# A hybrid encoder step on one core: the order of the transfers at the seam into the mixing stage, and the product W = T X in alternating column tiles

## The chip, the cores and the metric

The kernel runs on one core of a Trainium2 chip. It is written for the engines directly: each engine (TensorE or PE for matmuls, VectorE or DVE, ScalarE or ACT, GpSimd or POOL, SyncE or SP, which here only issues DMAs) has its own list of instructions and runs it in order. The engines meet at semaphores alone. The metric is the time of one execution on the device in microseconds (us); less is better.

## The reference, cut to what matters

One layer for 1024 prompt rows and 32 sample rows of width 1024. The part that the change touches:

```
h = RMSNorm(x);  p = h @ w_in          # q/kv latents, rwkv columns z, gate logits (2*D_MODEL)
branch A: multi-head latent attention over chunks
branch B: zm = z + (prev - z) * mu;  r, k, v, decay, a, g from zm
          per step: s = s*w + (s a) b + v k;  y = s r      # delta rule, 8 heads of 64
x = x + sum_n sigmoid(gate_n) * (branch_n @ w_out[n])
x = x + HierMoE(RMSNorm(x))            # top-1 of 4 groups, top-2 of 8 experts, 32 experts in all
outputs also: kv latents, rope keys, the state, the last projected row (shift)
```

## The kernel before, in words

The rows are cut into NT = 9 tiles of 128 (eight of the prompt, the ninth with the 32 sample rows). The stages follow each other: the inputs' projection (names a_), the mixing (b_, with some shared buffers r_), attention (c_), output projection and router (d_), experts (f_).

**Mixing.** The delta rule is solved in blocks: for each tile t and head, a triangular system is inverted by merging (levels 2 to 64; `low` and `merge`), giving T in `U`; then W = T X (`solved`), the new state (`state`) and the outputs (`outputs`). A loop over laps s = -1 to 9 runs three tiles at once in steps k = 0 to 11: features of tile s+1, the inverse of tile s, and right side, W, state and outputs of tile s-1. `solved(t)` stands at k = 2 of a lap.

Between these small pieces PE fills in the gate logits: 36 items q = 0 to 35, nine tiles for each of four column blocks, as 128x512 matmuls of `hT[q % 2]` and a weight block `wg[u % 2]` of 2 MB. How many go where is a table (`FILL_OF`). Six parts of item 0 run ahead of the turned heads of the last input tile. For each item q, SP stores the logits (`store_logits(q)`, after ACT copied them out of PSUM) and loads the `hT` of item q+2 into the buffer that item q has left (`load_hT(q + 2)`). So item 3 needs the load that follows `store_logits(1)` in SP's order.

**The seam.** SP's mixing list begins while the last input tile is still being stored. It loads `hT` 1 and `zm` 1; stores the last `zm` and turned heads, then the two last projected rows (`shift`, 128x14 elements of 4 bytes each); stores logits 0, loads `hT` 2; waits until all stores of the input stage have landed and tells POOL and DVE so (`inputs_over`); loads the second weight block `wg[1]`, which item 9 is the first to read; and copies rows of `x` into an unused part of `gate_d` (two copies in DRAM of 384 KB), to have numbers there. Only then come `store_logits(1)` and `load_hT(3)`.

**W = T X.** T has a left half of columns (rows 0 to 63 alone are not zero) and a right half. For the left one, PE runs eight matmuls on 64 rows of `U[t % 2]` into PSUM rows 0 to 63; then it waits for `lower_copied` and runs eight on all 128 rows of `U_right` into PSUM rows 64 to 127. ACT copies the lower part of `U_right` at k = 10 of the lap ahead (`copy_lower`); DVE writes its upper part. Each float32 matmul is two instructions in the trace.

The mixing's `state`, `outputs` and `right_side` are written so that a matmul for PSUM rows 0 to 63 and one for rows 64 to 127 follow each other in turn (`for q in HALVES`).

Of the kernel before, what the change touches and what calls it, by code (L numbers as in the profile page):

```python
# [23 lines left out]
ACT = mybir.ActivationFunctionType  # L24
AX = mybir.AxisListType.X

P = 128
# [101 lines left out]
def inputs_stage(nc, io, early, held, block):  # L129

    HK = H * QK // 2
    with ExitStack() as c:
# [68 lines left out]
        def store_zm(sp, t):  # L201
            sp.wait_ge(zm_ready, t + 1)
            sp.dma_start(io["zm_d"][t], zm[:]).then_inc(zm_stored, 16)
# [6 lines left out]
                    mm = pe.transpose(banks[b][0:QK, j * P:(j + 1) * P], qk[:, first + h + j, :], ident[:])  # L210
                mm.then_inc(qkT_done, 1)

        def store_last(sp):

            store_zm(sp, NT - 1)
            store_qk(sp, NT - 1)
            for g in range(2):
                sp.wait_ge(row_kept, g + 1)
                sp.dma_start(io["shift"][g], zlast[:, g, :]).then_inc(shift_stored, 16)

        def all_stored(sp):
# [8 lines left out]

        last = dict(sems=sems, over=inputs_over, mixed=(zm_ready, NT), z_copied=(z_copied, NG_Z * NT), z_done=(z_done, NG_Z * NT), zm_stored=(zm_stored, 16 * (NT - 1)),
                    kv_copied=(qkv_copied, turn(NT)), turned_copied=(qkT_copied, turns_before(NT)),
                    store=store_last, stored=all_stored, turn_heads=lambda pe: turn_heads(pe, NT - 1))

        @block.sync
        def _(sp):
# [381 lines left out]
def mixing(nc, io, early, held, inputs, hand_over, block):  # L618
# [10 lines left out]
    with ExitStack() as c:  # L629
# [42 lines left out]
        M = [sb(f"M{j}", [P, H, 2, 2 * P]) for j in range(2)]  # L672
        T = sb("T", [P, H, HALF_T])
        U = [sb(f"U{j}", [P, H, HALF_T]) for j in range(2)]
        U_right = sb("U_right", [P, H, HALF_T])
        ident64 = sb("ident64", [P, HALF_T])
        L = [sb(f"L{i}", [P, H, Q if i < 2 else HALF_T]) for i in range(4)]
# [25 lines left out]
        def after(eng, sem, n):  # L703

            if n > 0:
                eng.wait_ge(sem, n)
# [17 lines left out]
        def _(sp):  # L724
# [24 lines left out]
            load_hT(1)  # L749
            sp.wait_ge(*inputs["zm_stored"])  # L750
            load_zm(1)
            inputs["store"](sp)
            store_logits(0)
            load_hT(2)
            inputs["stored"](sp)
            load_wg(1)
            for n in range(2):
                sp.dma_start(io["gate_d"][LAST, DEC:, 2 * n:2 * n + 2, :], io["x"][LAST, DEC:, :].rearrange("p (a b) -> p a b", a=2)).then_inc(no_logits, 16)
            q = 1
            for s in range(-1, NT + 1):  # L760
                if s >= 2:
                    sp.wait_ge(out_ready, s - 1)
                    sp.dma_start(io["ob_d"][s - 2], y[:]).then_inc(ob_stored, 16)
                for _ in range(6):
                    if q < ITEMS and parts_upto(q + 1) <= fill_upto(s):
                        store_logits(q)
                        if q + 2 < ITEMS:
                            load_hT(q + 2)
                        if tile_of(q) == LAST and unit_of(q) + 2 < UNITS:
                            load_wg(unit_of(q) + 2)  # L770
                        q += 1
                if s + 3 < NT:
                    load_zm(s + 3)
                if s == LAST:
                    sp.wait_ge(bon_done, NT)
                    sp.wait_ge(v_turned, NT)
                    load_head(sp, io, early, 0, 0, early["head_in0"])
                    sp.wait_ge(state_out, 1)
                    sp.dma_start(io["wkv"][0], grown[:]).then_inc(state_stored, 16)
# [10 lines left out]
        @block.gpsimd  # L790
        def _(pool):
            pool.wait_ge(*inputs["z_done"])
            pool.memset(bias[:, 0:1], CENTRE)
            pool.memset(bias[:, 1:2], -CENTRE)
            pool.memset(one[:], 1.0).then_inc(set_done, 1)
            pool.wait_ge(inputs["over"], 1)
            pool.memset(L[2][:], 0.0)
            pool.memset(S[0][:], 0.0).then_inc(set_done, 1)

            pool.wait_ge(lora_done, 1)  # L800
            pool.wait_ge(v_copied, 1)
            pool.wait_ge(gram_copied, PAIRS)
            give_back(pool, inputs["sems"])
            prime(pool, next_ones)
# [198 lines left out]
        def _(act):  # L1003
# [59 lines left out]
            def copy_lower(t):  # L1063
                act.wait_ge(merged, NL * t + NL - 1)
                after(act, w_done, t)
                h = H // 2
                act.activation(U_right[HALF_T:, 0:h, :], U[t % 2][HALF_T:, h:, :], ACT.Copy)
                act.activation(U_right[HALF_T:, h:, :], U[t % 2][HALF_T:, 0:h, :], ACT.Copy).then_inc(lower_copied, 1)

# [59 lines left out]
        def _(pe):  # L1129
# [96 lines left out]
            def solved(t):  # L1226
                pe.wait_ge(x_copied, t + 1)
                pe.wait_ge(merged, NL * t + levels_of(t))
                pe.wait_ge(U_ready, TURNED * (t + 1))
                after(pe, y_copied, t)  # L1230
                for h in range(H):
                    cols = slice(h * RH, (h + 1) * RH)
                    mm = pe.matmul(banks[WY][0:HALF_T, cols], U[t % 2][0:HALF_T, h, :], X[0:HALF_T, cols], start=True, stop=True)
                if t < LAST:
                    pe.wait_ge(lower_copied, t + 1)
                    for h in range(H):
                        cols = slice(h * RH, (h + 1) * RH)
                        mm = pe.matmul(banks[WY][HALF_T:, cols], U_right[:, h, :], X[:, cols], start=True, stop=True)
                mm.then_inc(w_done, 1)

            def state(t):
# [1331 lines left out]
```

## Time and profile before

| | us |
|---|---|
| median of 3 runs | 1621.47 |
| lowest, highest | 1621.18, 1624.18 |
| the profiled execution | 1621.25 |
| its span, first to last instruction | 1619.4 |
| PE busy | 1498.9 (93%) |
| DVE busy | 857.0 (53%) |
| ACT busy | 445.2 (27%) |

The input stage takes the first 342 us, the mixing goes on to 898, attention to 1088, the output projection to about 1270, the experts to the end. A busy share is an average over stages with different limits; a wait of one engine costs only where the others wait for it in turn. DVE and ACT have idle time in all stages.

### The profile page before, as it was taken

How to read it: one execution, taken by the hardware profiler on the slowest of the kernel's cores; microseconds unless marked ns; L12 is line 12 of the kernel's file. 1: busy time of each engine (PE TensorE's matmuls, PEld its weight loads, DVE VectorE, ACT ScalarE, POOL GpSimd, SP SyncE). 2: the span in 40 equal slices, each digit the busy share in tenths (PEclk: the TensorE clock that was granted, in tenths of full speed). 3: DMA queues.
4: the chain of work that ended last, by engine and by line, in shares of the span. 5: the costliest groups of instructions: out<-in, count | busy, mean ns of one | idle time of the engine just before them, and what ended most of it. 6: DMA issues, size and time to landing. Idle time of an engine off the chain costs nothing. (4 is left out here: it accounts for less than half of the span.)

```text
span 1619.4 us, 38770 instructions
## 1 busy us (share of the span) xinstructions
PE 1498.9 (93%) x16352; PEld 1062.5 (66%) x16352; DVE 857.0 (53%) x1874; ACT 445.2 (27%) x882; POOL 102.1 (6%) x102
## 2 busy tenths in 40 slices
PE   6999999998999999999998699988999599999994
PEld 5888888864666666666666466653554477777772
DVE  3545554464666766767667566664767323222111
ACT  2222222241233233233231244434444211111110
POOL 0000000000000000000000000000000122233321
PEclk9999999998999999999999699998999699999998
DMA  9422221553142132211112434436963799999972
GB/s 334 177 91 97 90 91 64 197 176 127 60 130 89 63 114 74 78 65 66 60 59 63 117 84 91 91 75 249 371 217 130 277 316 338 343 352 359 349 242 45
DMA packets 101326, 259.55 MB, mean 160 GB/s; under 512 B 34240, under 2 KB 53328, under 8 KB 91824
## 3 DMA queue, kind: packets, MB, share of 16 engines
q1 hardware_dynamic: 93424, 239.92, 43.1%
q0 software_dynamic: 7744, 17.33, 4.5%
q8 instruction: 124, 2.03, 0.5%
q14 instruction: 34, 0.28, 0.0%
HBM read 205.32 MB, written 60.56 MB: 164 GB/s over the span
## 5 line engine op out<-in xcount | busy, mean ns | idle before, releaser
L560 PEld LDWEIGHTS a_ps<-a_hT,a_wz 128*128 128x128 f32 x1792 | 202.6, 192 | 6.2 <-issue 3.8
L560 PE MATMUL a_ps<-a_hT,a_wz 128*128 128x128 f32 x1792 | 204.1, 275 | 1.7 <-DMA a_wz<-w_z 1.7
L1981 PE MATMUL d_ps<-late,last_down 128*128 128x512 f32 x256 | 115.4, 598 | 1.5 <-DVE last_down L1745 0.8
L2347 DVE TENSOR_SCALAR f_y<-f_down,table 96x512 f32<-96x512 f32 x32 | 23.9, 747 | 116.7 <-PE f_down L2142 68.0
L2149 DVE COPY f_xT<-f_turned 128x384 f32<-128x384 f32 x32 | 17.8, 557 | 128.0 <-PE f_turned L2116 128.0
L1981 PEld LDWEIGHTS d_ps<-late,last_down 128*128 128x128 f32 x256 | 46.7, 190 | 51.5 <-issue 50.2
L868 DVE TENSOR_TENSOR b_M<-b_ps,r_causal 128x512 f32<-128x512 f32 x72 | 46.4, 686 | 58.6 <-PE b_ps L1209 58.1
L1506 ACT ACTIVATE late<-c_score,c_top 128x1024 f32<-128x1024 f32 (+8 forms) x72 | 50.6, 703 | 92.7 <-DVE c_top L1455 92.2
L1146 PE MATMUL b_ps<-r_wg,b_hT 128*128 128x512 f32 x128 | 64.2, 627 | 5.2 <-DMA b_hT<-hT_d 5.2
L1146 PE MATMUL b_ps<-r_wg,r_hT 128*128 128x512 f32 x128 | 63.0, 625 | 2.0 <-DMA r_hT<-hT_d 2.0
L1146 PE MATMUL b_ps<-b_wg,b_hT 128*128 128x512 f32 x128 | 63.3, 616 | 0.7 <-DMA b_hT<-hT_d 0.7
L1146 PE MATMUL b_ps<-b_wg,r_hT 128*128 128x512 f32 x128 | 63.1, 615 | 0.0
L2142 PE MATMUL f_down<-wd,f_midT 128*96 128x512 f32 x136 | 61.3, 593 | 1.8 <-DVE f_midT L2161 1.8
L1299 PE MATMUL b_solve<-b_L,b_U 64*64 64x32 f32 x1408 | 57.2, 222 | 5.6 <-DVE b_L L944 5.4
L2354 ACT ACTIVATE f_xT<-f_turned 128x384 f32<-128x384 f32 x32 | 15.7, 491 | 163.9 <-PE f_turned L2116 163.9
L1299 PEld LDWEIGHTS b_solve<-b_L,b_U 64*64 64x64 f32 x1408 | 51.2, 136 | 13.5 <-DVE b_L L944 6.5
L472 ACT ACTIVATE a_z<-a_ps 128x512 f32<-128x512 f32 (+1 forms) x36 | 19.6, 544 | 140.9 <-PE a_ps L560 134.1
L944 DVE TENSOR_TENSOR b_L<-b_solve,r_merge_mask 128x256 f32<-128x256 f32 x44 | 18.7, 424 | 72.4 <-PE b_solve L1283 72.4
L1283 PEld LDWEIGHTS b_solve<-b_T,b_M 64*64 64x64 f32 x1408 | 44.5, 135 | 18.4 <-issue 7.8
L1553 PE MATMUL c_turned<-c_ident,late 128*128 128x128 f32 (+1 forms) x304 | 49.9, 290 | 6.1 <-ACT late L1506 6.1
L2266 POOL DMA_INDIRECT out<-f_y,rows x32 | 46.3, 1446 | 138.9 <-DVE f_y L2347 135.1
L2372 ACT ACTIVATE f_y<-f_down,table 96x512 f32<-96x512 f32 x32 | 21.9, 684 | 120.1 <-PE f_down L2142 70.8
(373 smaller groups left out, 2924.0 us busy)
## 6 DMA issues: line engine op xcount, KB each, us to landing
wgu<-w_gate_up SPq DMA_DIRECT2D x15, 2048.0 KB
late<-w_gate_up SPq DMA_DIRECT2D x9, 2048.0 KB
wd<-w_down SPq DMA_DIRECT2D x17, 1024.0 KB
late<-w_down SPq DMA_DIRECT2D x10, 1024.0 KB, 31.9
r_hT<-hT_d SPq DMA_DIRECT2D x18, 512.0 KB, 4.0
b_hT<-hT_d SPq DMA_DIRECT2D x18, 512.0 KB, 4.0
gate_d<-b_logits SPq DMA_DIRECT2D x32, 256.0 KB, 2.6
late<-gate_d SPq DMA_DIRECT2D x8, 1024.0 KB, 5.9
```

Of the source, the lines that this page charges most:

```text
L560: mm = pe.matmul(banks[Z_BANKS[n % 2]][:, j * P:(j + 1) * P], wz[:, i, (g + j) * P:(g + j + 1) * P], hT[t % 2][:, i, :], start=(i == 0), s ...
L868: ins = dve.tensor_tensor(m[:, 2 * p + j], banks[(C0, C1)[j]][:].rearrange("p (a b) -> p a b", a=2), spread(causal[:].unsqueeze(1), [P, 2, ...
L1146: mm = pe.matmul(banks[FILLS[q % 2]][:], hT[q % 2][:, k, :], wg[u % 2][:, k, :], start=(k == 0), stop=(k == DC - 1))
L1283: mm = pe.matmul(solve[half, s // 4, s % 4 * Q:s % 4 * Q + Q], m[half, h, 0, half], left, start=True, stop=True)
L1299: mm = pe.matmul(out(1), u[half, s, :], lo[half, s, 0:Q], start=True, stop=True)
L1506: act.activation(probs[b][:, 0:width[s]], score[b][:].rearrange("p a n -> p (a n)")[:, 0:width[s]], ACT.Exp, bias=top[:, b:b + 1], accum_o ...
L1553: mm = pe.transpose(turned[banks_of(p)[n // 4]][0:m, n % 4 * P:(n % 4 + 1) * P], probs[b][:, n * P:n * P + m], ident[:])
L1981: mm = pe.matmul(banks[2 + u][:], oT[t % 2][:, HB * branch(u) + k, :], wo[:, HB * branch(u) + k, half(u)], start=(k == 0), stop=(k == HB - 1))
L2142: mm = pe.matmul(down[h][0:CAP, :], midT[b][:, k, :], wd[wb][:, k, 512 * h:512 * h + 512], start=(k == 0), stop=(k == FB - 1))
L2266: pool.indirect_dma_start(out_rows, bass.IndirectOffsetOnAxis(ap=rows[:, ORDER[e]:ORDER[e] + 1], axis=0), y[e % 2][:], None, bounds_check= ...
L2347: dve.tensor_scalar(y[e % 2][:, 512:], down[1][0:CAP, :], weights[:, ORDER[e]:ORDER[e] + 1], None, ALU.mult).then_inc(s["y_dve"], 1)
L2372: act.activation(y[e % 2][:, 0:512], down[0][0:CAP, :], ACT.Copy, scale=weights[:, ORDER[e]:ORDER[e] + 1]).then_inc(s["y_act"], 1)
```

## The change: what it does

SP's list at the seam is put in another order: the shift rows are stored behind `store_logits(0)` and `load_hT(2)`; `store_logits(1)` and `load_hT(3)` come ahead of `load_wg(1)`; and the two copies of `x` move to lap s = 1, behind its last load. The stored total and all bytes stay the same.

A new buffer `U_left` holds the left half of T as 128 rows of which the lower 64 are zero (POOL sets it once; ACT copies the upper part once a tile, ahead of its copies for `U_right`). W is then made of 128x64 column tiles from `U_left` and `U_right` in turn. The last tile keeps the short form.

```diff
-            inputs["store"](sp)
+            inputs["store_z"](sp)
+            inputs["store_heads"](sp)
             store_logits(0)
             load_hT(2)
+            inputs["store_row"](sp)
             inputs["stored"](sp)
+            store_logits(1)
+            load_hT(3)
             load_wg(1)
-            for n in range(2):
-                sp.dma_start(io["gate_d"][LAST, DEC:, 2 * n:2 * n + 2, :], io["x"][LAST, DEC:, :].rearrange("p (a b) -> p a b", a=2)).then_inc(no_logits, 16)
-            q = 1
+            q = 2
...
+                if s == 1:
+                    for n in range(2):
+                        sp.dma_start(io["gate_d"][LAST, DEC:, 2 * n:2 * n + 2, :], io["x"][LAST, DEC:, :].rearrange("p (a b) -> p a b", a=2)).then_inc(no_logits, 16)
...
+            pool.memset(U_left[:], 0.0)
...
+                act.activation(U_left[0:HALF_T, :, :], U[t % 2][0:HALF_T, :, :], ACT.Copy)
...
+                if t < LAST:
+                    pe.wait_ge(lower_copied, t + 1)
                 for h in range(H):
                     cols = slice(h * RH, (h + 1) * RH)
-                    mm = pe.matmul(banks[WY][0:HALF_T, cols], U[t % 2][0:HALF_T, h, :], X[0:HALF_T, cols], start=True, stop=True)
-                if t < LAST:
-                    pe.wait_ge(lower_copied, t + 1)
-                    for h in range(H):
-                        cols = slice(h * RH, (h + 1) * RH)
-                        mm = pe.matmul(banks[WY][HALF_T:, cols], U_right[:, h, :], X[:, cols], start=True, stop=True)
+                    if t == LAST:
+                        mm = pe.matmul(banks[WY][0:HALF_T, cols], U[t % 2][0:HALF_T, h, :], X[0:HALF_T, cols], start=True, stop=True)
+                        continue
+                    for q, u in zip(HALVES, (U_left, U_right)):
+                        mm = pe.matmul(banks[WY][q, cols], u[:, h, :], X[:, cols], start=True, stop=True)
```

SP's order at the seam, before. `b_hT1` and `r_hT0` are the two `hT` buffers, `b_wg1` is the second weight block, L219 the shift rows, L758 the copies of `x`:

```order
L199 DMA kT_d<-a_qkT 96x1024
L219 DMA shift<-a_zlast 128x14 x2
L742 DMA gate_d<-b_logits0 128x512
L727 DMA r_hT0<-hT_d 128x1024
L732 DMA b_wg1<-w_gates 128x8x512
L758 DMA gate_d<-x 96x1024 x2
L742 DMA gate_d<-b_logits1 128x512
L727 DMA b_hT1<-hT_d 128x1024
L742 DMA gate_d<-b_logits0 128x512
```

The same place in the changed kernel:

```order
L199 DMA kT_d<-a_qkT 96x1024
L742 DMA gate_d<-b_logits0 128x512
L727 DMA r_hT0<-hT_d 128x1024
L217 DMA shift<-a_zlast 128x14 x2
L742 DMA gate_d<-b_logits1 128x512
L727 DMA b_hT1<-hT_d 128x1024
L732 DMA b_wg1<-w_gates 128x8x512
L742 DMA gate_d<-b_logits0 128x512
```

The load of item 3's `hT` now stands ahead of the weight block, and the copies of `x` are gone from here.

PE's order at `solved` of the first tile, before:

```order
L1146 MATMUL b_ps7<-b_wg1,b_hT1 128x512 x3
L1233 MATMUL b_ps3<-b_X,b_U0 64x64 x8
L1238 MATMUL b_ps3<-b_X,b_U_right 64x64 x8
L1299 MATMUL b_solve<-b_L1,b_U1 64x32 x16
L1146 MATMUL b_ps7<-b_wg1,b_hT1 128x512 x2
```

And in the changed kernel, its first rows (the pair comes eight times, and then the merge's L1307 follows, which was L1299):

```order
L1153 MATMUL b_ps7<-b_wg1,b_hT1 128x512 x3
L1246 MATMUL b_ps3<-b_X,b_U_left 64x64
L1246 MATMUL b_ps3<-b_X,b_U_right 64x64
L1246 MATMUL b_ps3<-b_X,b_U_left 64x64
L1246 MATMUL b_ps3<-b_X,b_U_right 64x64
```

The sixteen matmuls stay sixteen; left and right now alternate.

## Rows read from the trace of the kernel before

**Rows 1.** The page, parts 1 and 2: busy shares, and the span in 40 slices

```profile
PE 1498.9 (93%) x16352; PEld 1062.5 (66%) x16352; DVE 857.0 (53%) x1874; ACT 445.2 (27%) x882; POOL 102.1 (6%) x102
DMA  9422221553142132211112434436963799999972
```

**Rows 2.** Timeline of PE, 364 to 379 us: start, length, line, idle before

```profile
363.79 4.88 PE L1146 MATMUL b_ps<-r_wg,r_hT 128*128 128x512 f32 x11
373.83 3.78 PE L1146 MATMUL b_ps<-r_wg,b_hT 128*128 128x512 f32 x4 [5.16 <-DMA b_hT<-hT_d]
```

**Rows 3.** Timeline of SP's DMA issues, 345 to 375 us

```profile
352.64 3.11 SPq L219 DMA_DIRECT2D shift<-a_zlast  x2
355.79 0.44 SPq L742 DMA_DIRECT2D gate_d<-b_logits  x1
356.27 0.44 SPq L727 DMA_DIRECT2D r_hT<-hT_d  x1
358.28 0.55 SPq L732 DMA_DIRECT2D b_wg<-w_gates  x1
358.88 1.30 SPq L758 DMA_DIRECT2D gate_d<-x  x2
361.95 0.33 SPq L742 DMA_DIRECT2D gate_d<-b_logits  x1
362.32 0.55 SPq L727 DMA_DIRECT2D b_hT<-hT_d  x1
369.33 0.32 SPq L742 DMA_DIRECT2D gate_d<-b_logits  x1
```

**Rows 4.** All loads of hT (L727), issue to landing: minimum, median, maximum

```profile
DMA to landing us min/median/max: 3.4/4.0/11.5
```

**Rows 5.** The same for the two stores of the shift rows (L219)

```profile
DMA to landing us min/median/max: 3.8/4.0/4.1
```

**Rows 6.** Windows: length, PE, PEld, DVE, ACT, POOL busy, granted clock, DMA share, GB/s

```profile
368.00:374.00 6.00, 0.84 (x3) 0.17 (x2) 3.55 (x6) 0.60 (x1) 0.00 (x0) 0.81 0.89 348
374.00:380.00 6.00, 6.00 (x12) 2.93 (x13) 0.00 (x0) 0.60 (x1) 0.00 (x0) 0.62 0.03 12
...
400.00:405.00 5.00, 5.00 (x23) 2.40 (x22) 1.24 (x3) 0.60 (x1) 0.00 (x0) 0.50 0.00 0
```

**Rows 7.** Timeline of PE, 380 to 432 us: logits item 4, and the first inverse

```profile
387.63 1.98 PE L1146 MATMUL b_ps<-r_wg,r_hT 128*128 128x512 f32 x4
...
397.19 1.12 PE L1283 MATMUL b_solve<-b_T,b_M 64*64 64x32 f32 x32 [1.60 <-DVE b_T L882]
```

**Rows 8.** Timeline of PE, 455 to 480 us: W, a merge, the state, a merge

```profile
463.31 1.14 PE L1233 MATMUL b_ps<-b_X,b_U 64*64 64x64 f32 x16
464.38 1.15 PE L1238 MATMUL b_ps<-b_X,b_U_right 128*64 128x64 f32 x16
465.46 1.45 PE L1299 MATMUL b_solve<-b_L,b_U 64*64 64x32 f32 x32
...
473.44 0.34 PE L1249 MATMUL b_ps<-b_W,b_tok 128*64 128x64 f32 x4
...
474.30 0.29 PE L1251 MATMUL b_ps<-b_tok 128*64 128x64 f32 x4
474.52 1.12 PE L1299 MATMUL b_solve<-b_L,b_U 64*64 64x32 f32 x32
```

**Rows 9.** Timeline of DVE, 455 to 512 us

```profile
460.66 0.42 DVE L944 TENSOR_TENSOR b_L<-b_solve,r_merge_mask 128x256 f32<-128x256 f32 x1 [3.99 <-PE b_solve L1283]
...
466.95 0.42 DVE L958 TENSOR_TENSOR b_T<-b_T,b_solve 128x256 f32<-128x256 f32 x1 [2.75 <-PE b_solve L1299]
```

**Rows 10.** Timeline of ACT, 495 to 525 us

```profile
507.45 0.41 ACT L1067 ACTIVATE b_U_right<-b_U 64x256 f32<-64x256 f32 x1
...
511.31 0.58 ACT L1057 ACTIVATE b_X<-b_ps 128x512 f32<-128x512 f32 x1
```

**Rows 11.** Timeline of PE, 509 to 530 us: the next W

```profile
522.17 1.14 PE L1233 MATMUL b_ps<-b_X,b_U 64*64 64x64 f32 x16
```

**Rows 12.** SP's waits from 900 us on: total, times, longest

```profile
SPq L2197 <- PE f_down L2142: 194.0, 24, 10.8
```

More of the change, by code:

```diff
@@ L211, in turn_heads, with store_last_row @@
                 mm.then_inc(qkT_done, 1)
-        def store_last(sp):
-            store_zm(sp, NT - 1)
-            store_qk(sp, NT - 1)
+        def store_last_row(sp):
             for g in range(2):
@@ L232, in inputs_stage @@
                     kv_copied=(qkv_copied, turn(NT)), turned_copied=(qkT_copied, turns_before(NT)),
-                    store=store_last, stored=all_stored, turn_heads=lambda pe: turn_heads(pe, NT - 1))
+                    store_z=lambda sp: store_zm(sp, NT - 1), store_heads=lambda sp: store_qk(sp, NT - 1),
+                    store_row=store_last_row, stored=all_stored, turn_heads=lambda pe: turn_heads(pe, NT - 1))
         @block.sync
@@ L674, in mixing @@
         U = [sb(f"U{j}", [P, H, HALF_T]) for j in range(2)]
+        U_left = sb("U_left", [P, H, HALF_T])
         U_right = sb("U_right", [P, H, HALF_T])
```

## The prediction

> **What bounds the kernel now.** I read the page first: PE is busy 93% of the span, DVE 53%, and the DMA engines are near their limit only in the first slice and the last quarter [rows 1]. So an edit counts where PE waits, where PE works at the lower clock, or where PE's own work gets shorter. Then I looked in PE's timeline for waits at the places of the edits. At the seam PE stops for 5.16 us, from 368.67 (363.79 + 4.88) to 373.83, and what ends the stop is the load of `hT` for logits item 3 [rows 2]. SP's timeline tells why it is late: it was issued at 362.32, behind the 2 MB weight block (358.28) and the two copies of `x` (358.88) [rows 3], and took 11.5 us, the longest of all loads of this kind, where the median takes 4.0 [rows 4]. Around it the DMA engines were 89% busy; once it had landed, 3% [rows 6]. It was 0.5 MB at the end of a queue of 3.4 MB.
>
> The stop has a second price. In 374 to 380 the granted clock is 0.62 [rows 6]. With two levels, full and half, that means that PE was at half clock (1.2 GHz) for (1 - 0.62) x 2 x 6 = 4.56 us, in which it did 2.28 us of work.
>
> In the mixing's laps PE's work sets the pace. W takes from 463.31 to 465.46, 2.15 us for 32 instructions, or 67 ns each [rows 8]. The state, a few steps later, has as many instructions (four groups of eight) of the shape 128*64 on 64 columns, with the two column tiles in turn: from 473.44 to the merge at 474.52, 1.08 us, 34 ns each with entry and exit [rows 8]. That is the nearest thing to the new W.
>
> **The change part by part.**
>
> *hT of item 3 ahead of the weights.* Its issue still waits for ACT's copy of item 1's logits; SP stored those at 361.95 [rows 3]. What now stands ahead of it on SP? The two shift stores: 3.11 us to issue [rows 3], and at most 4.1 us to land [rows 5]. Logits 0 and `hT` 2, which waited behind them until 355.79, go first, at 354.8 or so; the shift stores begin at about 355.7, the second at 357.4, landed at about 361.5. The wait for all stores ends there, some 3.3 us later than now (the weight block, right behind it, was issued at 358.28), but still 0.4 us ahead of the logits it could hold up. Others who wait for it: POOL's memsets, and through them the first inverse at 397.19 [rows 7], with over 30 us of cover. So the issue of `hT` 3 stays at 362.4. Landing: with the shortest load, 365.8; with the longest, 373.9; I take the median of 4.0, 366.4, since what made the long one long is now behind it. PE wants it at 368.67. The stop of 5.16 us goes.
>
> *The clock.* Without the stop PE has no gap over 1 us there, so the stretch at half clock behind it should go as well: 2.28 us. Seam: 5.16 + 2.28 = 7.4 us. Lower end: the clock falls anyway, 5.2. Upper end: another half-clock stretch goes too, 10.4 (below).
>
> What comes late next? DVE did nothing from 374 to 380 [rows 6]: it had finished tile 0's features and waited for PE, so it is no new bound. The weight block is issued at about 363 and lands some 12 us later, at 375; PE's first matmuls with it stand just ahead of the first W at 463.31. Item 4's `hT` is issued behind item 2's logits (369.33) and behind the block in the queue, and should land by 377; PE began item 4 at 387.63 [rows 7] and will now at 380.2. A cover of 3 us, the thinnest here; without it up to 3 us of the gain would go.
>
> *The copies of x.* They move to the end of lap 1, near 505 us, behind a load of `hT` and of `zm`. They take 1.30 us to issue [rows 3]; in that slice the DMA engines are at two tenths [rows 1]. Nothing waits for them before the stage ends. Cost nothing; if they got in the way of a load, as at the seam, their 1.5 MB read and written would cost about 4 us at 348 GB/s [rows 6].
>
> *W in column tiles.* Eight tiles, each from 2.15 to 1.08 us: 1.07 x 8 = 8.6 us less PE work. The bounds: at the pace inside the state, 28 instructions from 473.44 to 474.30 or 31 ns each [rows 8], W takes 0.98 us, a gain of 9.4; at 67 ns, the pace of one column tile alone (L1238, [rows 8]), the gain is nothing.
>
> Is it on the path? Behind W stands the merge at 465.46. It needs DVE's product that began at 460.66 and took 0.42 [rows 9]: over 4 us early, so it can start 1.07 us sooner. DVE's next step idles 2.75 us for that merge [rows 9] and moves with it. The state at 473.44 has 8 us of cover behind ACT's copy of W. All later steps of a lap hang on PE's pieces, so the lap moves as a whole.
>
> *ACT's new copy.* 64x512 elements a tile. Half that size takes 0.41, and 512 elements a row in 128 rows 0.58 [rows 10]: I take 0.58, eight times, 4.6 us of ACT work. It delays the copy of X at 511.31 [rows 10]; PE's W wants that at 522.17 [rows 11], 10 us later. PE's wait for `lower_copied` now stands ahead of both halves, but ACT makes that copy before the copy of X, for which W waits anyway. Cost nothing; without the cover 0.6 a tile.
>
> Sum: 7.4 + 8.6 = 16.0 us. The profiled execution took 1621.25, 0.2 below the median of 1621.47. 1621.25 - 16.0 = 1605.25; I say 1605.3.
>
> By the Trainium skill, "TensorE: Matmul & The Clock Gate", Part 3 ("The mechanism"), a weight load overlaps running matmuls only when its row group differs. Both halves of W use all row groups, so by that rule nothing would overlap, and the sum would be 7.4. The trace speaks against it: the state's column tiles on all 128 rows run at half the time of one tile alone.
>
> **The rivals.**
>
> *The pairs don't pair.* Column tiles in turn would take 67 ns for each instruction, as a tile alone does. For it: W's two halves stream the same X in turn, which the state doesn't do, so the state is a likeness and no proof. Against it: the shapes and tile positions are the state's own. W stays at 2.15 us; 1621.25 - 7.4 = 1613.9. Chance 8%.
>
> *The stop moves.* The wait for all stores holds `hT` 3 up, or item 4 waits behind the weights, by about 3 us, with some half clock behind it. The seam gives about 3 instead of 7.4: 1609.7. Chance 10%.
>
> *A second half-clock stretch goes.* At 397.19 PE waits 1.60 us for the first inverse [rows 7], and shortly after the clock is 0.50 for 5 us [rows 6]: 2.5 us lost, about 3 with its edges. The gap stays in the changed kernel, so I keep the loss. But all work shifts against the clock's changes; here, or where a later stage starts out of idle time at half clock, 3 us more may go: 1602.3. Chance 10%.
>
> *Given back by the experts.* There the DMA engines are at nine tenths [rows 1]. If the stream of weights ran by its own time, an earlier PE would only wait for it: 1621. Against it: SP waits 194.0 us in 24 waits for PE's down projections before it issues [rows 12], so the stream moves with PE. Chance 3%.
>
> *Slower.* The laps begin with small matmuls and short waits, and it was behind such a stretch that the clock fell at 400. Now W's 2 us are 1, and less PE work separates those stretches. If the clock fell in a lap as it did at 400, a lap would lose about 3 us more. It takes seven laps (21) to undo the 16.0 and end measurably above; all eight (24) give 1629.3. Against it: those are the eight laps' full count, and the work that replaces W is denser, not sparser. Chance 2%.
>
> **How the numbers follow.** The forecast, 1605.3, has 67%, and its own range is 1602.5 to 1608.5: W at 0.98 to 1.2 us, the seam between 5.2 and 7.6, and the clock of later stages by 1 us either way. The range goes from 1600.8 (the second stretch gone, and 1.5 us at a later start) to 1612 (a stop that moved, with more half clock); no pairing, given back and slower, 13%, lie outside. A measurement of this kernel can tell about 0.2%, or 3.2 us, from no change. All cases but the last two end below 1618.2: faster 0.95, same 0.03, slower 0.02.
>
> **What would show it.** PE should run through 368 to 374 without a wait for a DMA, at clock 1.00 until the first inverse's gap, which should be at about 390. W's start and the start of the merge behind it should be 1.1 us apart, not 2.15. Item 4's first matmul must not wait. DVE's busy time stays, ACT's grows by 4.6 us. It is wrong if PE's waits for `hT` come back a few us later, or if the laps don't get shorter by 1.07 us each.

## The result: 1606.61 us, and the profile after

| | before | after |
|---|---|---|
| median of the runs, us | 1621.33 | 1606.61 |
| lowest, highest | 1619.19, 1624.18 | 1604.47, 1609.76 |
| the profiled execution | 1621.25 | 1604.47 |
| its span | 1619.4 | 1602.6 |

The ratio of after to before is 0.9905, with a 95% interval of 0.9884 to 0.9925: 14.7 us less, from four runs of each. The kernel got faster, as forecast; the forecast was 1605.3 us, 1.3 below the median. The span of the profiled execution, which the traces below divide up, fell by 16.8.

The busy line of the page of after (busy us, share of the span, instructions) answers to [rows 1]:

```profile
PE 1489.6 (93%) x16352; PEld 1055.7 (66%) x16352; DVE 857.1 (53%) x1874; ACT 449.1 (28%) x890; POOL 102.7 (6%) x103
```

PE does the same 16352 instructions in 9.3 us less; DVE's time is unchanged, and ACT's eight new copies add 3.9.

**The seam.** SP's DMA issues in after (start, length, line, tiles), which answer to [rows 3]:

```profile
354.84 1.10 SPq L217 DMA_DIRECT2D shift<-a_zlast  x2
361.17 0.33 SPq L742 DMA_DIRECT2D gate_d<-b_logits  x1
361.55 0.42 SPq L727 DMA_DIRECT2D b_hT<-hT_d  x1
362.01 1.65 SPq L732 DMA_DIRECT2D b_wg<-w_gates  x1
```

PE's timeline in after, at item 3's first matmul and item 4's, for [rows 2] and the first line of [rows 7]:

```profile
367.73 1.88 PE L1153 MATMUL b_ps<-r_wg,b_hT 128*128 128x512 f32 x4
...
379.13 1.98 PE L1153 MATMUL b_ps<-r_wg,r_hT 128*128 128x512 f32 x4
```

There is no wait in brackets any more. Four matmuls of item 3 take 1.88 us where they took 3.78. The windows of after (length; PE, PEld, DVE, ACT, POOL busy; granted clock; DMA share; GB/s), for [rows 6]:

```profile
368.00:374.00 6.00, 6.00 (x24) 3.31 (x23) 2.77 (x5) 2.21 (x4) 0.00 (x0) 1.00 0.98 317
374.00:380.00 6.00, 6.00 (x31) 3.44 (x30) 2.61 (x6) 2.01 (x4) 0.00 (x0) 1.00 0.17 67
388.00:394.00 6.00, 4.80 (x80) 3.41 (x82) 3.38 (x6) 0.60 (x1) 0.00 (x0) 1.00 0.02 4
```

The DMA engines are busier in 368 to 374 than before (0.98 against 0.89), yet PE works through, because the load it wants is no longer behind the others. The clock stays at 2.4 GHz, also through the gap ahead of the first inverse, which is still there (third window).

**W.** PE's timeline in after, at the first W, for [rows 8]:

```profile
451.25 0.27 PE L1246 MATMUL b_ps<-b_X,b_U_left 128*64 128x64 f32 x1
451.26 0.27 PE L1246 MATMUL b_ps<-b_X,b_U_right 128*64 128x64 f32 x1
451.36 0.22 PE L1246 MATMUL b_ps<-b_X,b_U_left 128*64 128x64 f32 x1
451.37 0.22 PE L1246 MATMUL b_ps<-b_X,b_U_right 128*64 128x64 f32 x1
...
452.33 1.12 PE L1307 MATMUL b_solve<-b_L,b_U 64*64 64x32 f32 x32
```

A left and a right instruction start within 10 ns of each other, and a pair follows a pair every 50 to 60 ns inside the run. (128*64 is the part of the array that an instruction uses, rows by columns; the text calls this its form.) From W's start to the merge: 1.08 us, where it was 2.15. So it is in seven of the eight tiles. In the eighth, in a lap with little other work for PE, the merge comes 1.73 us after W's start (855.29 less 853.56), since it now waits for a product of DVE; in the kernel before it came after 2.13, without a wait.

```profile
855.29 1.12 PE L1307 MATMUL b_solve<-b_L,b_U 64*64 64x32 f32 x32 [0.58 <-DVE b_L L950]
```

Here is how far ahead of the kernel before the same work starts, by the two profiles' timelines:

| start of | before | after | earlier by |
|---|---|---|---|
| the last input tile | 286.5 | 285.7 | 0.78 |
| tile 0's products, PE | 383.58 | 375.07 | 8.51 |
| the work behind the first inverse's clock stretch | 406.10 | 394.38 | 11.72 |
| state, tile 0 | 473.44 | 459.98 | 13.46 |
| state, tile 1 | 532.0 | 517.5 | 14.52 |
| state, tile 7 | 876.6 | 858.0 | 18.61 |
| attention's scores | 909.06 | 891.77 | 17.29 |
| the experts' first tile | 1280.23 | 1263.59 | 16.64 |

So the seam gave 7.7 (8.51 less the 0.78 with which the profile came out of the input stage, which no edit touches). The half-clock stretch of [rows 6] at 400 is gone in this profile: 3.2. Seven W gave about 1.07 each; of the eighth's, 0.28 is left at its state. The gain is 18.6 at the last of these states, although a half-clock stretch behind the wait for `hT` at 579, which is new, took 1.7 on the way. From there to the experts two more us are lost; the clock is at half for longer there than in the kernel before (34 us between 870 and 909, against 27 between 890 and 922). What comes out is 16.8.

### The profile page after: what moved, and what is told of

Same layout as the page of the kernel before. It is cut to its first block and busy times, and to the rows that moved or that the text cites. A ratio compares the mean times of both kernels' runs of the same rounds, so it can differ in the third digit from the quotient of the medians.

```text
span 1602.6 us, 38780 instructions
## 1 busy us (share of the span) xinstructions
PE 1489.6 (93%) x16352; PEld 1055.7 (66%) x16352; DVE 857.1 (53%) x1874; ACT 449.1 (28%) x890; POOL 102.7 (6%) x103
## 5 line engine op out<-in xcount | busy, mean ns | idle before, releaser
L1307 PE MATMUL b_solve<-b_L,b_U 64*64 64x32 f32 x1408 | 56.0, 220 | 5.9 <-DVE b_L L950 5.9
L1307 PEld LDWEIGHTS b_solve<-b_L,b_U 64*64 64x64 f32 x1408 | 50.3, 134 | 13.7 <-DVE b_L L950 7.2
```

The source lines that it names most:

```text
L1307: mm = pe.matmul(out(1), u[half, s, :], lo[half, s, 0:Q], start=True, stop=True)
```

## The experiments

All ratios are to the kernel before, run beside each group of experiments (its medians there were 1621.71, 1621.99 and 1620.65 us), with a 95% interval. In the diffs the changed kernel is the starting point unless it is said otherwise; `...` stands for what is left out.

**1. The parts apart.** The seam alone (W and its buffer as before):

```diff
-    for q, u in zip(HALVES, (U_left, U_right)):
-        mm = pe.matmul(banks[WY][q, cols], u[:, h, :], X[:, cols], start=True, stop=True)
+    mm = pe.matmul(banks[WY][0:HALF_T, cols], U[t % 2][0:HALF_T, h, :], X[0:HALF_T, cols], start=True, stop=True)
...
+        mm = pe.matmul(banks[WY][HALF_T:, cols], U_right[:, h, :], X[:, cols], start=True, stop=True)
...
-    act.activation(U_left[0:HALF_T, :, :], U[t % 2][0:HALF_T, :, :], ACT.Copy)
```

> The changed kernel with W in its old form: only SP's order at the seam differs from the kernel before. Theory A (the two parts add): PE has no wait for a DMA at 368 us, the products of tile 0 come 7.4 to 7.7 us earlier against the same point of the input stage, each W still takes 2.15 us, and the time is 7.4 below the kernel before, or some 3 more where the half-clock stretch near 400 us is absent too: ratio 0.9935 to 0.9955. Rival B (the seam carries all of the gain, what W saves is given back): ratio 0.990, as with both parts.

The tiles alone (the kernel before, with the edits of W):

```diff
+    act.activation(U_left[0:HALF_T, :, :], U[t % 2][0:HALF_T, :, :], ACT.Copy)
...
+    for q, u in zip(HALVES, (U_left, U_right)):
+        mm = pe.matmul(banks[WY][q, cols], u[:, h, :], X[:, cols], start=True, stop=True)
```

> The kernel before with W in column tiles in turn and nothing else. Theory A: the stop of 5.2 us at 369 stays, each of eight W takes 1.08 instead of 2.15 us, and the time falls by 8.6 us: ratio 0.9945 to 0.995. Rival B (the laps take it back in waits for DVE and ACT): ratio 0.998 to 1.000, and PE's waits for the merge's operands grow by 8 us in sum.

And the changed kernel once more, beside them:

> The changed kernel once more, for a second profile and a time beside its parts. Theory A: the sum of the two parts, 16 us below the kernel before, 0.990. On the half-clock stretch near 400 us of the kernel before, which the first profile of the changed kernel did not have: if the seam's order took it away, it is absent again (clock 1.00 in 380 to 410); if it depends on where a run's clock changes happen to fall, it may be back in this profile, for 3 us.

Measured: the seam alone 1611.42, ratio 0.9949 (0.9933 to 0.9965); the tiles alone 1615.82, 0.9961 (0.9942 to 0.9981); both 1606.18, 0.9903 (0.9876 to 0.993). The two gains, 0.51% and 0.39%, add up to 0.90%; both together give 0.97%. The tiles alone gained a little less than expected (0.9945 to 0.995), within the noise.

The traces part the two more sharply than the times do. With the seam alone, the work at 406 starts 8.57 us earlier (0.81 of it from the input stage) and the state of tile 7 9.06: the laps give nothing. With the tiles alone, the states of tiles 0 to 7 start 0.77, 1.83, 2.90, 4.06, 5.13, 6.13, 7.18 and 7.47 us earlier: nearly 1.07 a tile, but 0.29 for the last, where the merge waits for DVE as in after. Its stop at the seam is still there; here PE's timeline of the tiles alone:

```profile
373.86 3.78 PE L1149 MATMUL b_ps<-r_wg,b_hT 128*128 128x512 f32 x4 [5.87 <-DMA b_hT<-hT_d]
```

The second execution of the changed kernel answers the question of its expectation: the half-clock stretch behind the first inverse is back (391 to 396, 1.7 us lost), so the order at the seam had not taken it away.

No run leaves the shift rows where they were. SP stored logits 1 at 361.17 in after and at 361.95 before, which is the 0.78 of the input stage, so the place of those rows shows no effect on the load; it is not tested by itself.

**2. Is it the turn, or the form?** W from the same two buffers, but all of the left half, then all of the right one:

```diff
-    for h in range(H):
-        for q, u in zip(HALVES, (U_left, U_right)):
+    for q, u in zip(HALVES, (U_left, U_right)):
+        for h in range(H):
             mm = pe.matmul(banks[WY][q, cols], u[:, h, :], X[:, cols], start=True, stop=True)
```

> The changed kernel, but W's sixteen matmuls in another order: eight from U_left, then eight from U_right, all on 128 rows. Theory A (the alternation of the column tiles is what makes them overlap): 67 ns for each instruction again, W 2.15 us, time 8.6 us above the changed kernel, ratio to before 0.995 to 0.996. Rival C (one tile shape for both halves is what counts, since the old W changed from 64*64 to 128*64): W stays near 1.1 us and the ratio 0.990.

And in turn, but the left half with its 64 rows, so without the zeros, the buffer and ACT's copy:

```diff
-    for q, u in zip(HALVES, (U_left, U_right)):
-        mm = pe.matmul(banks[WY][q, cols], u[:, h, :], X[:, cols], start=True, stop=True)
+    mm = pe.matmul(banks[WY][0:HALF_T, cols], U[t % 2][0:HALF_T, h, :], X[0:HALF_T, cols], start=True, stop=True)
+    if t < LAST:
+        mm = pe.matmul(banks[WY][HALF_T:, cols], U_right[:, h, :], X[:, cols], start=True, stop=True)
...
-    act.activation(U_left[0:HALF_T, :, :], U[t % 2][0:HALF_T, :, :], ACT.Copy)
```

> The changed kernel with W's matmuls in turn, but the left half from the 64 rows of U itself, as in the kernel before: no U_left and no copy of ACT. Theory A (two tiles overlap only when both have one form, 128 rows by 64 columns): each change between 64*64 and 128*64 costs, W takes 2.15 us or more, up to twice that with 15 changes of form where there was one; time 8.6 us or more above the changed kernel. Rival E (the alternation of the column tile alone makes them overlap): W 1.08 us and 0.990, and the copy into U_left was not needed.

Measured: not in turn 1614.43, 0.9953 (0.9936 to 0.997); 64 rows in turn 1652.56, 1.0173 (1.0146 to 1.0201), the only kernel of the study slower than before. PE's timeline of the one that is not in turn:

```profile
455.13 0.97 PE L1248 MATMUL b_ps<-b_X,b_U_left 128*64 128x64 f32 x13
...
455.99 0.22 PE L1248 MATMUL b_ps<-b_X,b_U_right 128*64 128x64 f32 x1
455.99 0.22 PE L1248 MATMUL b_ps<-b_X,b_U_left 128*64 128x64 f32 x1
...
456.11 0.92 PE L1248 MATMUL b_ps<-b_X,b_U_right 128*64 128x64 f32 x13
456.96 1.12 PE L1309 MATMUL b_solve<-b_L,b_U 64*64 64x32 f32 x32
```

1.83 us, in all eight tiles; theory A had expected 2.15 and rival C 1.1, and neither came. So of the 1.07 us a tile, 0.75 come only with the turn. The other 0.32 come without it, but not all of them by the one form: where the halves meet, six left and right instructions start within 0.23 us (455.88 to 456.11), which at 67 ns each would be 0.40. That leaves some 0.15 for the form. PE's timeline of the one with 64 rows:

```profile
456.02 0.33 PE L1239 MATMUL b_ps<-b_X,b_U 64*64 64x64 f32 x2
456.27 0.33 PE L1241 MATMUL b_ps<-b_X,b_U_right 128*64 128x64 f32 x2
...
460.32 0.96 PE L1302 MATMUL b_solve<-b_L,b_U 64*64 64x32 f32 x14
```

4.30 us, the last of it at half clock; the W of four tiles at full clock take 4.10 or 4.11. Each two instructions take 0.257 us here, against 0.134 at the 67 ns of one tile alone: each change between the forms 64*64 and 128*64 adds some 0.12 us, sixteen times. Against the pace in turn (0.068) it would be 0.19. The Trainium skill says in "TensorEngine Tiling (Array Packing)", Key Properties, that a change of the tiling mode drains the engine; the trace agrees, with these 0.12 us a change. That is what the lower 64 rows of zeros buy: half of the left tile's work is multiplying zeros, and it is cheaper than changing form. Side by side, W takes 2.15 us with two forms one after the other, 1.83 with one form one after the other, 4.11 with two forms in turn, and 1.08 with one form in turn.

From W's start to the merge, the eight tiles sum to 33.9 us where they are 9.3 in after, 24.6 more, but the span is 48.5 longer than after's (1651.1 against 1602.6). The rest is the clock. Windows of the kernel with 64 rows, behind its first two W (columns as above; the granted clock is the third number from the right):

```profile
460.00:466.00 6.00, 6.00 (x39) 3.75 (x40) 3.08 (x7) 2.41 (x3) 0.00 (x0) 0.50 0.00 0
524.00:528.00 4.00, 4.00 (x36) 2.39 (x33) 2.83 (x7) 1.77 (x2) 0.00 (x0) 0.58 0.02 6
```

Stretches at 1.2 GHz like these stand behind seven of the eight W; the last runs on into attention's start. Over the span, work done at half clock cost 47.0 us where it cost 22.9 in after: 24.1 more, and 24.6 + 24.1 = 48.7 accounts for the 48.5. (The two overlap a little, where the end of a W ran at half clock.)

**3. What held the load up?** First the weight block alone ahead of item 3's load, then the two copies of `x` alone ahead of it, then the copies at the seam but behind everything:

```diff
             inputs["stored"](sp)
+            load_wg(1)
             store_logits(1)
             load_hT(3)
-            load_wg(1)
```

> The changed kernel with the 2 MB weight block ahead of the store of logits 1 and the hT load of item 3; the copies of x stay in lap 1. Theory A (what held the load was the whole queue of 3.4 MB): with 2 MB in front of it, at some 350 GB/s, it lands about 1 us after PE wants it at 367.7, so PE waits 0 to 2 us. Rival D (the weight block alone was the cause): PE waits about 5 us there, as in the kernel before, and the time is 7 us above the changed kernel.

```diff
             inputs["stored"](sp)
+            for n in range(2):
+                sp.dma_start(io["gate_d"][LAST, DEC:, 2 * n:2 * n + 2, :], io["x"][LAST, DEC:, :].rearrange("p (a b) -> p a b", a=2)).then_inc(no_logits, 16)
             store_logits(1)
...
-                if s == 1:
-                    for n in range(2):
-                        sp.dma_start(io["gate_d"][LAST, DEC:, 2 * n:2 * n + 2, :], io["x"][LAST, DEC:, :].rearrange("p (a b) -> p a b", a=2)).then_inc(no_logits, 16)
```

> The changed kernel with the two copies of x ahead of the store of logits 1 and the hT load of item 3, and the weight block behind it. Theory A: 1.5 MB read and written take some 4.3 us at 350 GB/s, the load lands near 367, and PE waits 0 to 1 us. Rival D': copies inside DRAM go far below that rate (their issue to landing was 10.4 to 12.3 us behind the weights), and PE waits 3 us or more.

```diff
             load_hT(3)
             load_wg(1)
+            for n in range(2):
+                sp.dma_start(io["gate_d"][LAST, DEC:, 2 * n:2 * n + 2, :], io["x"][LAST, DEC:, :].rearrange("p (a b) -> p a b", a=2)).then_inc(no_logits, 16)
...
-                if s == 1:
-                    for n in range(2):
-                        sp.dma_start(io["gate_d"][LAST, DEC:, 2 * n:2 * n + 2, :], io["x"][LAST, DEC:, :].rearrange("p (a b) -> p a b", a=2)).then_inc(no_logits, 16)
```

> The changed kernel with the copies of x at the seam again, right behind the weight block, so that only the hT loads from item 4 on stand behind them. Theory A: item 4's load lands by about 376 to 378 and PE begins item 4 at 379.1, so it waits for nothing or for less than 1 us; same time as the changed kernel. Rival F (that cover is gone): PE waits at 379 us for 1 to 3 us.

Measured: weights ahead 1616.23 us, ratio 0.9953 (0.9926 to 0.9979); copies ahead 1605.83, 0.9898 (0.9871 to 0.9926); copies behind 1609.58, 0.9907 (0.9879 to 0.9936). SP's issues and PE's wait, with the weights ahead:

```profile
360.16 0.55 SPq L732 DMA_DIRECT2D b_wg<-w_gates  x1
362.02 0.99 SPq L727 DMA_DIRECT2D b_hT<-hT_d  x1
...
372.93 3.78 PE L1153 MATMUL b_ps<-r_wg,b_hT 128*128 128x512 f32 x4 [4.57 <-DMA b_hT<-hT_d]
```

and with the copies ahead:

```profile
359.76 1.23 SPq L759 DMA_DIRECT2D gate_d<-x  x2
361.66 0.43 SPq L727 DMA_DIRECT2D b_hT<-hT_d  x1
...
367.78 1.88 PE L1152 MATMUL b_ps<-r_wg,b_hT 128*128 128x512 f32 x4
```

The block alone brings back a wait of 4.57 us, and the half clock behind it (371 to 379); with the copies alone ahead PE does not wait. In both kernels the DMA engines are over 90% busy from 362 to 374, so it is not the traffic as such. It is what stands ahead in the queue. How long item 3's load took from issue to landing (the last number) in after, with the copies ahead and with the weights ahead, and then the block of the last one:

```profile
b_hT<-hT_d SPq DMA_DIRECT2D x1, 512.0 KB, 4.3
b_hT<-hT_d SPq DMA_DIRECT2D x1, 512.0 KB, 5.9
b_hT<-hT_d SPq DMA_DIRECT2D x1, 512.0 KB, 10.9
b_wg<-w_gates SPq DMA_DIRECT2D x1, 2048.0 KB, 10.8
```

The copies do slow the load: it lands at 367.6 (361.66 + 5.9), near the 367 of theory A, and PE wants it at 367.78. That no wait shows is a matter of 0.2 us. With the weights ahead it lands at 372.9, 1.9 us behind the block (360.16 + 10.8 = 371.0); the wait is near rival D's 5 us and outside theory A's 0 to 2. But here the block was issued 1.9 us later than in the kernel before (358.28), because the stores that it waits for end later. So the 4.57 us are not the block's share of the old 5.16. In the kernel before, with the copies between the two, the load landed 3.8 us behind the block (358.28 + 11.7 = 370.0, and 373.8). An estimate from these rows: the block alone, issued at 358.28, would have let the load land at about 371.9, a wait of some 3.2 us, and the copies added the other 1.9. No run has that order.

The block is slow to go through the queue. Its load, issue to landing (minimum, median, maximum), in the kernel before:

```profile
DMA to landing us min/median/max: 11.1/11.7/11.7
```

That is 2 MB in some 11.7 us, 180 GB/s, in each of three places. Around the one at 594 us, the DMA engines moved only 2.7 MB in 12 us, and the block still took 11.1. So the block's time can't be had from the rate of 348 at which the prediction priced the copies. The Trainium skill's "DMA: Bandwidth & Descriptors", "Queues, rings and completion order", says that each DMA engine takes descriptors in ring order; with the block ahead the trace agrees, since the load of 0.5 MB lands 1.9 us behind it.

With the copies behind the weights no new wait appears at item 4, but again only just: its load, issued at 372.14, took 9.9 us and landed at 382.0, and PE began the item at 382.35. In after the load took 7.9 and had 2.3 us to spare. Its span is 7.3 us longer than after's: 3.2 of them are lost in the input stage, whose program is the same, and 3.2 behind the first inverse, by the clock. Its median is 3.0 higher, with intervals that overlap.

**4. What is left: the gap ahead of the first inverse, and the late hT in the laps.** Two parts of the logits are moved from step 7 of lap -1 to step 0 of lap 0, behind the first products, so that PE has work in the gap:

```diff
         def fill_of(s, k):
+            if (s, k) in ((-1, 7), (0, 0)):
+                return 0 if s < 0 else 4
             return (3 if k < NL else 2) if s < 0 else FILL_OF[k]
```

> The changed kernel with two parts of the gate logits (1.7 us of PE) moved from step 7 of lap -1 to step 0 of lap 0, in front of the first inverse, where PE waits 1.60 us for DVE's transposed T. Theory A (DVE has 5.5 us of idle time ahead of the products, so its chain moves up with PE): the wait of 1.6 us at 388 goes, the second half-clock stretch behind it, seen in most profiles, goes too (3.3 us or 1.7), and the time falls by 2 to 4 us. Rival G: the values or rows come to wait for DVE or ACT instead, no gain.

In the laps SP issues the load ahead of the store, so that it isn't behind the store's wait for ACT's copy:

```diff
-                        store_logits(q)
                         if q + 2 < ITEMS:
                             load_hT(q + 2)
+                        store_logits(q)
```

> The changed kernel with each hT load of the laps issued ahead of the store of the same item's logits, not behind it, so that it doesn't wait for ACT's copy. Theory A: the load for item 18 is issued at 573.4 instead of 575.0, PE's waits of 1.8 us there and 0.9 us near 713 go, and with the first of them the half-clock stretch that three profiles show right behind it (580 to 590, 1.3 to 1.7 us); 2 to 4 us faster. Rival H: the stores, now behind 0.5 MB, hold ACT's next copy and PE up: no gain or a loss.

Both:

> Both edits of the two kernels before this one together. Theory A: they add, 4 to 8 us below the changed kernel (ratio to before 0.985 to 0.988). Rival: the clock falls elsewhere for as much, and only the 4.3 us of waits are gained.

Measured: fill moved 1603.20, 0.9888 (0.9869 to 0.9908); load first 1604.39, 0.9899 (0.9881 to 0.9918); both 1599.38, 0.9866 (0.985 to 0.9883), four runs within 1598.55 to 1600.80. The last is the fastest kernel of the study, 21 us below the kernel before that ran beside it. It is some 6 or 7 us below the changed kernel, which did not run beside it; the intervals of the ratios just touch (0.9883 against 0.9876 in experiment 1), and those of each edit alone overlap the changed kernel's. What the single edits gain is seen in the traces, not proven by the times. PE's timeline at the first inverse, changed kernel, then both edits:

```profile
388.68 1.12 PE L1291 MATMUL b_solve<-b_T,b_M 64*64 64x32 f32 x32 [1.60 <-DVE b_T L888]
```

```profile
383.65 3.70 PE L1155 MATMUL b_ps<-r_wg,r_hT 128*128 128x512 f32 x8
387.28 1.12 PE L1293 MATMUL b_solve<-b_T,b_M 64*64 64x32 f32 x32
```

The wait of 1.60 is gone. At lap 2 the changed kernel waits for an `hT`; with load first this wait is shorter, but not gone, where theory A had it gone. The one of 0.87 near 713 is gone. Changed kernel, then load first:

```profile
579.09 2.52 PE L1153 MATMUL b_ps<-r_wg,r_hT 128*128 128x512 f32 x4 [1.80 <-DMA r_hT<-hT_d]
```

```profile
584.24 1.98 PE L1153 MATMUL b_ps<-r_wg,r_hT 128*128 128x512 f32 x4 [1.00 <-DMA r_hT<-hT_d]
```

What the clock did behind these gaps is in the windows of PE alone at three places of the laps (busy, granted clock, DMA share, GB/s): the changed kernel's second execution, fill moved, load first, and both.

```profile
388.00:400.00 12.00, 10.77 (x128) 0.86 0.20 68
444.00:452.00 8.00, 7.57 (x82) 0.79 0.74 228
578.00:590.00 12.00, 10.12 (x213) 0.86 0.79 232
```

```profile
388.00:400.00 12.00, 11.47 (x147) 1.00 0.22 69
444.00:452.00 8.00, 8.00 (x64) 0.79 0.93 315
578.00:590.00 12.00, 10.04 (x154) 0.86 0.86 269
```

```profile
388.00:400.00 12.00, 9.88 (x86) 0.72 0.06 11
...
578.00:590.00 12.00, 11.00 (x252) 1.00 0.72 196
```

```profile
388.00:400.00 12.00, 11.47 (x147) 1.00 0.21 69
444.00:452.00 8.00, 7.82 (x105) 1.00 0.80 250
578.00:590.00 12.00, 11.48 (x161) 1.00 0.75 223
```

A clock of 0.86 over 12 us is (1 - 0.86) x 2 x 12 = 3.4 us at half clock, which does 1.7 us of work. With the gap filled the first place is clear. The third place is clear with load first, but it was also clear in six of the twelve profiles with the old order of load and store, the kernel before among them, whose wait there was 2.0 us; so it isn't shown that the earlier load did it. Both edits together have the only profile of the study without half clock from 342 to 869 us; from there, at the end of the mixing, they too run at half clock.

The middle place belongs to neither edit, but the traces show what stands ahead of it. The merge there breaks off halfway, and PE idles without waiting for anything that the profile shows; in fill moved:

```profile
442.89 0.71 PE L1309 MATMUL b_solve<-b_L,b_U 64*64 64x32 f32 x17 [1.36 <-issue]
```

In ten of the fourteen profiles this merge is lengthened so, by 0.3 to 1.4 us, and in seven of them the clock falls within 6 us behind it; in the four where it runs through in 1.12 us, it doesn't. What breaks it is open.

**5. ACT's cover.** The claim that ACT's new copy costs nothing, with three more of them behind it:

```diff
     act.activation(U_left[0:HALF_T, :, :], U[t % 2][0:HALF_T, :, :], ACT.Copy)
+    for j in range(3):
+        act.activation(spare[j][0:HALF_T, :, :], U[t % 2][0:HALF_T, :, :], ACT.Copy)
```

> The changed kernel with three more copies of 64x512 on ACT beside the one into U_left, into spare buffers that nobody reads: 1.8 us more ACT work in each of eight tiles. Theory A (that copy stands in 10 us of cover): X and the lora inputs come 1.8 us later, PE does not wait for them, the time is that of the changed kernel within 1 us, 0.990. Rival I (ACT's chain at the lap's start is near the limit): up to 1.8 us a tile, 14 us in all, and waits of PE for ACT in its list.

Measured: 1610.57, 0.9936 (0.9916 to 0.9956), 4.4 us above the changed kernel of experiment 1, with intervals that overlap; theory A had said within 1 us. ACT's timeline of this kernel:

```profile
500.43 1.65 ACT L1076 ACTIVATE b_spare<-b_U 64x512 f32<-64x512 f32 x3
502.09 0.41 ACT L1077 ACTIVATE b_U_right<-b_U 64x256 f32<-64x256 f32 x1
```

The three copies take 1.65 us a tile, 12.1 more of ACT's time in all (461.2 against 449.1), and don't show in the laps: from the work at 458.4 of the kernel before to that at 813.4, this kernel gains 5.16 us (6.03 to 11.19), and after 5.20 (12.06 to 17.26). PE has no wait for ACT that after hasn't. What differs in the two profiles is again the clock, by 3.2 us behind the first inverse and 1.7 at 448. So the cover held in the laps; whether all of the 4.4 us in the medians is the clock's, these runs leave open.

## Why the prediction was right, point by point

*The stop at the seam goes.* Right, with its mechanism: once the load is ahead of the block, PE has no wait there. The prediction had the issue at 362.4, and it was 361.55, or 362.3 with the 0.78 of the input stage. The stores of the shift rows took 1.10 us to issue, not the 3.11 of [rows 3], and the wait for all stores had ended by 360.16 (experiment 3), not at 361.5.

*The clock behind it.* Right: 1.00 in both windows, and the seam as a whole gave 7.7 where 7.4 were forecast (7.73 in after, 7.76 with the seam alone). The three profiles with the stop (before, tiles alone, weights ahead) all are at half clock from 371 or 372 to 379 or 380; of the eleven without it none is.

*Whose fault the stop was.* The prediction said of the load: "It was 0.5 MB at the end of a queue of 3.4 MB". (The 3.4 leave out the 0.25 MB of logits between.) Experiment 3 bears this out in the order of things: the load lands behind the block, and later still with the copies between; the larger part of the stop, about 3 of the 5 us by the estimate there, was the block's. What the prediction didn't have is the block's own rate: it took 11 to 13 us wherever it stood, longer than 2 MB at 348 GB/s. The price of the copies, "about 4 us at 348 GB/s", was not needed for the sum; in the one run with them ahead of the load they cost it 1.6 us (5.9 against 4.3).

*Item 4's thin cover of 3 us.* It held: the load landed at 376.8, and item 4 began at 379.13, without a wait, where 377 and 380.2 were forecast. With the copies put back it held by 0.3 us only.

*W.* Right to the hundredth: 1.08 us, the state's own time, in seven of eight tiles; in the last the merge behind it came 1.73 us after W's start. The Trainium skill's rule in "TensorE: Matmul & The Clock Gate", Part 3 ("The mechanism"), that a weight load overlaps only where its row group differs, would have left W at 2.15; the trace speaks against it, since both halves use all rows and W took half the time. The nearest row of the same shape and turn was the better guide than the rule. Experiment 2 adds what the prediction had not priced: most of the gain (0.75 of 1.07) is the turn, and the turn pays only with one form, since with mixed forms W takes nearly twice the old time.

*The lap moves as a whole.* Right for most tiles (1.06 to 1.07 from state to state in after and with the tiles alone). The exception is the last tile. "All later steps of a lap hang on PE's pieces" was read from the first W, where DVE's product for the merge was over 4 us early; in the last lap PE comes to wait 0.58 us for that product, and 0.28 of the 1.07 are left. So the eight W were worth about 7.8 us, not 8.6. PE's waits for a late `hT`, at 579 and 713, of 1.80 and 0.87 us, were there before too, of 2.0 and 0.7.

*ACT.* Its busy time grew by 3.9 us where 4.6 were forecast, and the cover of 10 us at the copy of X held, even for four copies.

*The second half-clock stretch.* "The gap stays in the changed kernel, so I keep the loss" was the choice for the sum, with 10% on its going. In the profiled execution it went (3.2 us), though the gap was there. In all, 12 kernels or executions were profiled with the gap, and 10 of them show a stretch at half clock behind it (1.7 to 3.4 us of work lost); of the two with the gap filled, none. This speaks for the gap as what leads to it, most times, though two profiles are few; the seam edits don't decide it. The same execution had a new stretch at 580 (1.7) and lost more at attention's start. The terms that the prediction set against each other at "1 us either way" were each larger, and nearly cancelled. Single executions of the changed kernel also spread over 15.6 us in experiment 1. So that 1605.3 stands 1.3 from the median is in part luck; what shows the mechanism is the starts in the traces.

*The rivals.* The pairs do pair; 1613.9, the price of the other case, is near what the kernel with W not in turn took (1614.43), though there W took 1.83 and not 2.15, which should have given 2.6 less; part of this nearness is chance. The stop did not move. Nothing was given back: the experts start 16.64 us earlier, and the last of their tiles still does 16.66. *Slower* had named its mechanism, a clock that falls lap after lap behind sparse small matmuls, "it takes seven laps". That is what the kernel with 64 rows did, in seven laps; it took a W of four times the new one's length to get there.

## What to carry to other kernels

On one queue, look at what stands ahead of the load that is wanted next: behind the 2 MB block the load of 0.5 MB took 10.9 us instead of 4.3, so issue the small and urgent one first. A change of order that shows no wait may still have used up the cover; compare the landing with the moment at which the data is wanted. Where short matmuls write the two halves of the PSUM rows, give both the same form, with zeros if need be, and alternate them; alternating with mixed forms took W to nearly twice its old time. Check the last lap by itself: with less other work there, what was covered in the others may come to bind. A stop of PE can cost more than itself: behind the stop of 5.16 us 2.3 more went at half clock, and behind the gap of 1.60 in most profiles 1.7 to 3.4. So after the largest stop is gone, the next ones are worth a try.

## What the runs showed of the hardware that was not expected

- A change between the forms 64*64 and 128*64 costs about 0.12 us, sixteen of them in a W that took 4.11 us at full clock.
- The weight block of 2 MB took 10.7 to 13.1 us in all kernels, 160 to 196 GB/s, while the loads of 0.5 MB took 4.0 in the median. The two copies of `x` landed after 4.0 us in the median where nothing stood ahead of them at the seam, and after 10.4 to 12.3 behind the block.
- The same two DMAs took SP 3.11 us to issue in one place and 1.10 in another (shift rows), and the copies of `x` 1.30 and 3.23. Nothing in the traces says what sets it.
- PE breaks off in the middle of a merge for up to 1.36 us, in some executions and not in others, and the profile shows nothing that it waits for.
- The same program varies by more than its laps do: the changed kernel's six runs in experiment 1 lie between 1598.72 and 1614.33, while its two profiled spans are 1602.6 and 1604.7. Both edits of experiment 4 together had the narrowest spread, 2.3 us in four runs.
